# A changed order in the forgetting attention, and ScalarE's function table asked for ahead of two kinds of loops

## What is computed

```python
# forgetting attention: 16 heads of 64, q and k normalised, a decay c added to the logits
q = rms_norm(q.reshape(B, S, FOX_HEADS, FOX_HD), q_g).transpose(0, 2, 1, 3)
k = rms_norm(k.reshape(B, S, FOX_HEADS, FOX_HD), k_g).transpose(0, 2, 1, 3)
log_f = jax.nn.log_sigmoid(fz.astype(f32) + fgate_b.astype(f32))
c = jnp.cumsum(log_f, axis=1).transpose(0, 2, 1)
logits = jnp.einsum('bhqd,bhkd->bhqk', q[:, :, lo:hi], k[:, :, :hi]).astype(f32) * scale
logits = logits + c[:, :, lo:hi, None] - c[:, :, None, :hi]
probs = jax.nn.softmax(jnp.where(mask, logits, -jnp.inf), axis=-1)
outs.append(jnp.einsum('bhqk,bhkd->bhqd', probs.astype(v.dtype), v[:, :, :hi]))
# PEER: the same for all 16384 experts u here, the gates are 0 for those not chosen
act = jax.nn.gelu(jnp.einsum('td,ted->te', ht, u[et]), approximate=False)
return jnp.einsum('te,ted->td', gt * act, v[et])
# feed-forward of the last block
zc = zc + conv_w[tap] * zp[:, tap:tap + S]
gate, val = jnp.split(zc, 2, axis=-1)
return (jax.nn.silu(gate) * val) @ w_down
```

## Time and profile before

| | |
|---|---|
| median of 3 runs | 2532.29 us |
| the profiled execution's own time | 2528.75 us |
| its span, first to last instruction | 2527.0 us |
| TensorE busy | 2401.2 us, 95% |
| VectorE busy | 1634.5 us, 65% |
| ScalarE busy | 1286.7 us, 51% |
| GpSimd busy | 1003.7 us, 40% |
| mean granted clock of TensorE | 0.966 |
| ACT_TABLE_LOAD | 152, of 1.283 us each |

### The profile page before, as it was taken

The page is one execution under the profiler, slowest core; times in us unless marked ns, Lnnn a source line. Parts: engine busy times, 40 slices in busy tenths (PEclk is TensorE's granted clock), DMA queues, the critical chain, the costliest instruction groups (busy, mean ns, idle before and its releaser), DMA issues.

```text
span 2527.0 us, 51551 instructions
## 1 busy us (share of the span) xinstructions
PE 2401.2 (95%) x18346; PEld 2184.2 (86%) x18346; DVE 1634.5 (65%) x3049; ACT 1286.7 (51%) x1698; POOL 1003.7 (40%) x950
## 2 busy tenths in 40 slices
PE   6789999999999999998999989999999999899989
PEld 6779998999988888795899989998888888888987
DVE  5651898677788755422229967778886552334985
ACT  5434555555444444464355555554444544565654
POOL 4526787544333100031278874343330003654330
PEclk9889999999999999996899999999999999999999
DMA  4314555554555566551155545555555664444554
GB/s 145 105 45 142 158 167 165 159 159 157 162 168 165 171 193 196 155 162 42 59 149 175 175 150 166 165 156 165 166 168 177 192 193 141 127 119 134 171 158 150
DMA packets 106103, 383.61 MB, mean 152 GB/s; under 512 B 12433, under 2 KB 12705, under 8 KB 105633
## 3 DMA queue, kind: packets, MB, share of 16 engines
q1 hardware_dynamic: 104400, 379.13, 49.2%
q10 hardware_dynamic: 1616, 3.33, 0.4%
HBM read 381.37 MB, written 1.05 MB: 151 GB/s over the span
## 4 chain that ended last, share of the span: by engine, by line
PE 67%; POOL 14%; issue 13%; DVE 3%; ACT 2%; DVEq 0%; POOLq 0%; ACTq 0%
POOL w_lo L360 13%; PE bank L1565 10%; PE bank L1567 10%; PE bank L1566 10%; PE bank L1476 9%; PE bank L1477 8%; PE bank L1479 8%; PE bank L1739 4%; PE bank L1445 1%; PE bank L1806 1%; PE bank L1811 1%; DVE big L890 1%; ACT w_hi L462 0%; PE bank L1818 0%; PE bank L1638 0%
## 5 line engine op out<-in xcount | busy, mean ns | idle before, releaser
L462 ACT ACTIVATE w_hi<-ring 128x1024 fp32r<-128x1024 f32 x719 | 756.5, 1057 | 715.5 <-PE bank L1567 422.0
L360 POOL TENSOR_TENSOR w_lo<-ring,w_hi 128x1024 fp32r<-128x1024 f32 x281 | 702.6, 2517 | 965.0 <-ACT w_hi L462 963.7
L1476 PE MATMUL bank<-x_hi,w_hi 128*128 128x256 f32 x3328 | 961.3, 289 | 50.8 <-POOL w_lo L360 30.3
L1477 PE MATMUL bank<-x_hi,w_lo 128*128 128x256 f32 x3328 | 947.0, 285 | 0.0
L1479 PE MATMUL bank<-x_lo,w_hi 128*128 128x256 f32 x3256 | 925.8, 284 | 0.0
L855 DVE TENSOR_TENSOR w_lo<-ring,w_hi 128x1024 fp32r<-128x1024 f32 x438 | 539.3, 1232 | 261.1 <-ACT w_hi L462 255.9
L1476 PEld LDWEIGHTS bank<-x_hi,w_hi 128*128 128x128 f32 x3328 | 645.4, 194 | 66.3 <-issue 25.9
L1477 PEld LDWEIGHTS bank<-x_hi,w_lo 128*128 128x128 f32 x3328 | 645.8, 194 | 0.0
L1479 PEld LDWEIGHTS bank<-x_lo,w_hi 128*128 128x128 f32 x3256 | 629.8, 193 | 0.0
L1565 PE MATMUL bank<-w_hi,x_hi 128*128 128x512 f32 x1112 | 440.4, 396 | 5.6 <-DVE x_lo L862 5.6
L1567 PE MATMUL bank<-w_lo,x_hi 128*128 128x512 f32 x1112 | 434.5, 391 | 0.0
(11 more groups left out here) (253 smaller groups left out, 2190.7 us busy)
## 6 DMA issues: line engine op xcount, KB each, us to landing
ring<-u_dram SPq DMA_DIRECT2D x256, 512.0 KB, 3.7
ring<-v_dram SPq DMA_DIRECT2D x256, 512.0 KB, 3.7
ring<-up_dram SPq DMA_DIRECT2D x44, 512.0 KB, 3.7
ring<-wq_dram SPq DMA_DIRECT2D x32, 512.0 KB, 3.6
ring<-sb_in_dram SPq DMA_DIRECT2D x31, 512.0 KB, 3.7
ring<-od_in_dram SPq DMA_DIRECT2D x25, 512.0 KB, 3.6
ring<-down_dram SPq DMA_DIRECT2D x22, 512.0 KB, 3.6
ring<-ev_in_dram SPq DMA_DIRECT2D x21, 512.0 KB, 3.7
```

The source lines that it names most:

```text
L360: pool.tensor_tensor(w_lo[:, k % RING, :], ring[:, k % RING, :], w_hi[:, k % RING, :].bitcast(F32), ALU.subtract).then_inc(g["lo_pool"], 1)
L462: A(w_hi[:, k % RING, :], ring[:, k % RING, :], ACT.Copy).then_inc(g["w_hi_done"], 1)
L1476: mm(dst, hi[:, rows[c]], xh[:, c, :], start=(c == 0), stop=False)
L1477: mm(dst, lo[:, rows[c]], xh[:, c, :], start=False, stop=False)
```

## The change

It has four parts. First, `nc.scalar.preload_act_table` asks for the table set of Gelu in front of each loop of u, and for that of Silu in front of the feed-forward's first unit. Second, the eight slices of q and k are squared, summed and rooted in groups of 3, 3, 2 and 0 instead of 2, 2, 2 and 2. Third, TensorE waits in each `scores(j)` for the slices that this pair reads, where it waited for all eight in front of `fox()`. Fourth, in a pair TensorE turns its two heads ahead of the mix of the pair before, where it mixed first.

```diff
--- before.py
+++ after.py
@@ -48,6 +48,9 @@
 D_FF = 2816
 FC = D_FF // P
 FAR = 1e33
+
+
+SUM_GROUPS = [(0, 1, 2), (3, 4, 5), (6, 7), ()]
 
 
 G_EV, G_PEER0, G_OD, G_PEER1, G_MIX2, G_FFN2 = range(6)
@@ -519,6 +522,8 @@
 
                 loops = units // UNITS
                 highs(n[0] + 2)
+                if func != ACT.Copy:
+                    nc.scalar.preload_act_table(func)
                 if loops:
                     with act.Fori(0, loops) as i:
                         for q in range(UNITS):
@@ -738,11 +743,11 @@
             A(o_z[2], o_z[1], ACT.Ln, bias=1.0).then_inc(g["od_z_log"], 1)
             act.wait_ge(g["units_out"], u[0])
             for j in range(4):
-                for s in (2 * j, 2 * j + 1):
+                for s in SUM_GROUPS[j]:
                     A(o_sq[:, s * 512:(s + 1) * 512], o_qk[:, s * 512:(s + 1) * 512], ACT.Square).then_inc(g["od_sq"], 1)
                 unit(token_major(o_v, D, j), view=lambda s: b3(s, TB))
-                roots([(o_n[:, s * 512:(s + 1) * 512], bank[4 + s % 4][:, :]) for s in (2 * j, 2 * j + 1)], HD,
-                      "od_log", "od_root", 2 * j, "od_sum")
+                roots([(o_n[:, s * 512:(s + 1) * 512], bank[4 + s % 4][:, :]) for s in SUM_GROUPS[j]], HD,
+                      "od_log", "od_root", 3 * j, "od_sum")
             highs(n[0] + 3)
             fox()
             others(8)
@@ -798,6 +803,7 @@
                 A(f_sil[m % 3], f_zc[m % 3][:, 0:T], ACT.Silu).then_inc(g["ff_silu"], 1)
 
             highs(n[0] + 4)
+            nc.scalar.preload_act_table(ACT.Silu)
             z_out(0)
             loops = (FC - 1) // UNITS
             with act.Fori(0, loops) as i:
@@ -1797,6 +1803,7 @@
                 qk = b3(o_n, 16)
 
                 def scores(j):
+                    pe.wait_ge(g["od_qk_ready"], 4 + j // 2 + 1)
                     if j >= 2:
                         pe.wait_ge(g["fox_pt_act"], j - 1)
                         pe.wait_ge(g["fox_pt_dve"], j - 1)
@@ -1841,11 +1848,11 @@
                 for j in range(FH // 2):
                     if j + 1 < FH // 2:
                         scores(j + 1)
+                    turn(2 * j)
+                    turn(2 * j + 1)
                     if j:
                         mix(2 * j - 2)
                         mix(2 * j - 1)
-                    turn(2 * j)
-                    turn(2 * j + 1)
                 back(0)
                 mix(FH - 2)
                 mix(FH - 1)
@@ -1869,10 +1876,9 @@
             one_unit(features, 1)
             for j in range(4):
                 token_unit()
-                for s in (2 * j, 2 * j + 1):
+                for s in SUM_GROUPS[j]:
                     pe.wait_ge(g["od_sq"], s + 1)
                     head_sums(s, o_sq, "od_sum", "od_log")
-            pe.wait_ge(g["od_qk_ready"], 8)
             pe.wait_ge(g["od_bias_ready"], 1)
             pe.wait_ge(g["units_out"], u[0])
             fox()
```

## The result

The changed kernel took 2512.45 us (median of 7 runs, 2503.59 to 2516.38) beside 2527.84 us of the kernel before (7 runs, 2519.72 to 2537.94). The ratio is 0.9931 (95% interval 0.9914 to 0.9949), 17.4 us less (13 to 22), where 12.4 less were forecast; the two medians alone are 15.4 us apart. The sign, the size within the range and the place of most of it came out; two terms of the sum did not.

The account below looks back on a forecast made before the run. TensorE, busy 95% of the span, was taken as the bound. Hand-over 2.4, feed-forward 1, start of fox 3.8, clock 1.5 and turn 3.7 sum to 12.4 us less: 2520 us against the median of 2532.29, range 2496 to 2534.

Parts of the forecast that it names:

- Start of fox: Ahead of fox: regrouped slices leave no root behind the last unit, so TensorE starts 3.8 us earlier (2 to 5.0).
- Clock: In fox: with a smaller gap ahead, first scores run at 2.4 GHz, then it falls; 1.5 us (-1 to 3.8).
- the first rival: In fox: the clock stays up throughout, gaining 21 us in place of 1.5, so 2500 us; chance 0.12.
- the thin start: In fox's first pairs: after two scores TensorE waits for mask and exponential, so the clock was expected to fall early.
- Turn ahead of mix: In fox: a mix covers the 0.74 us wait for turned heads' copies ahead of five scores; 3.7 us (0 to 4.5).
- 2.4 from the hand-over: Hand-over to VectorE in u: nearly a whole table load, 1.2 us, saved once per layer; 2.4 us (0 to 2.6).
- 0 from the rest: Both halves of u: no gain, as VectorE's experts hold the turned slots and TensorE has no gap in the second half.
- The last rival: In u: GpSimd's low parts meet VectorE's two-input operations more often, six more per layer, so 2543 us; chance 0.06.
- Feed-forward: Feed-forward loop: table loads go, but VectorE's convolution and GpSimd's low part need the same time; 1 us (0 to 5.7).
- VectorE doesn't bind: In u and feed-forward: VectorE's chain moves forward with the feed, gaps go, 15.3 us more, 2505 us; chance 0.09.
- the order of fox changes little: In fox: regrouping or turn order brings nothing, only table loads count, about 2529 us; chance 0.10.

Follow-up runs that it names:

- e4: Kernel before with only the turn of a pair put ahead of the mix of the pair before: 2523.76 us, ratio 0.9982.
- e7: Changed kernel with ScalarE's exponentials of the gates after the 28th unit of u instead of the 27th: 2513.99 us, ratio 0.9948 to the kernel before.
- e8: Changed kernel with the gates' exponentials one unit later and TensorE doing 29 units ahead of the turned slots instead of 28: 2506.69 us, ratio 0.9918.
- e5: Kernel before with half of VectorE's 32 products at L1111 left out in each layer: 2518.73 us, ratio 0.9956.
- e6: Changed kernel with half of VectorE's 32 products at L1111 left out in each layer: 2494.95 us, ratio 0.9869 to the kernel before.
- e12: Changed kernel with the third tap of the feed-forward's convolution cut to 8 of 256 columns: 2502.87 us in a single execution.
- e3: Kernel before with only the slice groups of 3, 3, 2 and 0 and the later waits in scores: 2522.06 us, ratio 0.9974.
- e9: Changed kernel with fox's product of q and k over all 128 rows instead of 64: 2518.29 us, ratio 0.9958 to the kernel before.
- e10: Changed kernel with 24 products of bf16 zeros per pair added in fox: 2521.63 us, ratio 0.9970 to the kernel before.

## Why the prediction was right, and where it failed

The time came out within the range, and the term for fox by the mechanism that was forecast. Of the table loads neither term came out: that of u was half of what was measured and put in the wrong place, that of the feed-forward had the wrong sign.

**Start of fox, 3.8 forecast: right, 4.1.** TensorE's position relative to the kernel before was -2.44 us ahead of the sums, so 1154.19 would have been 1151.75, and it is 1147.62. The estimate of 1150.4 for the end of the last unit was 2.9 us too late, of which 2.4 us are the earlier arrival; and into time in which ScalarE waits for the sums fell 0.5 us of the added operations.

**Clock, 1.5: right, 1.5.** From the first scores to the first turn it was 7.5 us and is 5.3, 2.3 less. The rise behind fox takes 0.8 back. The forecast that the clock falls early and stays down held, and so did the reason to give the first rival only 0.12. But the thin start isn't its cause: in the changed kernel the clock fell 3 us after the first scores began, while the first two scores still ran without a gap (5.28 of 5.30 us busy) and before TensorE waited for mask and exponential.

**Turn ahead of mix, 3.7: right, 4.6.** Each of the five waits was worth 0.92 us of the period and not the 0.74 of the idle time that the timeline names. Rows of TensorE that stand back to back overlap (in e4 1163.97 and 1.54 us, and the next row at 1165.31), and rows across a wait don't, so the idle time named in a row is less than what a wait adds to the starts. The prediction should have gone by the starts.

**Sum of fox:** 4.1 + 2.3 + 4.6 - 0.8 = 10.2 us, against 9.0.

**u, 2.4 from the hand-over and 0 from the rest: the size was too small and the place was wrong.** The whole is 5.5 us. The hand-over gave 0.2 us per layer (TensorE's gap of 1.88 us from start to start became 1.70). The chain behind the load at 449.09, GpSimd's two low parts, its copies and VectorE's tables, ended only 0.2 us later than another: VectorE's low parts also wait until ScalarE has taken out a unit that TensorE finishes just then. In the changed kernel that unit binds:

```profile
457.90 0.60 ACT L533 ACTIVATE big<-bank 128x512 f32 x1 [1.91 <-PE bank L1485]
```
```profile
458.72 2.37 DVE L861 TENSOR_TENSOR w_lo<-ring,w_hi 128x1024 fp32r<-128x1024 f32 x2 [0.98 <-ACT big L533]
```

That is 0.22 us from the end of the unit to the low part. Before, the unit was out at 460.78, and the low part started at 461.18, 0.40 us behind it. The prediction had counted a load as being in series with a gap because it stood in front of it. The other 2.5 us per layer are from VectorE's chain, which I had taken as fixed. The last rival named just this mechanism, a GpSimd low part beside a two-input operation, and asked how many meetings there are; it came out with the other sign. The number of low parts from scores to slots is the same, 55, but they lie elsewhere. In layer 0, L1111's 32 products take 50.6 us instead of 54.7, the four comparisons at L1105 13.5 instead of 10.3, and the small steps at L1098 and L1117 1.4 less. VectorE's groups in the same stretch of the changed kernel, where the last line is that of the comparisons:

```profile
L1117 DVE TENSOR_TENSOR sco<-sco,big 128x256 f32<-128x256 f32 x32 | 50.6, 1650 | 0.1
...
L1111 DVE TENSOR_TENSOR sco<-big,iota 128x2048 f32<-128x2048 f32 x4 | 13.5, 3368 | 0.1
```

The groups alone can mislead: in the eight layers without the preload the products take 52.5 to 59.2 us and the comparisons 10.3 to 12.7, but the chains all take 175.5 to 176.4. That one such meeting lengthens the chain by its own price is shown by e7 and e8, that the chain sets TensorE's time by e5 and e6. That meetings also explain the 2.5 us of the preload is argued from these groups. Why just this change of pace is favourable isn't shown: it is where the low parts happen to fall, and the sign was luck. The Trainium skill ("SBUF — State Buffer", section *SBUF: two separate sides*) speaks of such a lock for the whole instruction. The 2.15 us for a low part of about 2.4 agree with it. The 1.28 us for a load and no drain held as well: the exponential at 420.90 starts 1.30 us after the start of its load at 419.60. The 2.66 us of the Trainium skill ("ScalarE: Activation LUTs", section *What ACT_TABLE_LOAD costs*) are not seen.

**Feed-forward, +1: wrong in sign, -0.7.** That VectorE binds was right. What I overlooked is that it then isn't neutral when the low parts come. Each unit has one low part of GpSimd, and it costs VectorE about 2 us wherever it falls: 2.82 us instead of 0.73 at L1388 (now L1394), or 3.81 instead of 1.91 at L1394 (now L1400). VectorE's own operations make some 4.2 us, with the meeting 6.27, and TensorE needs 5.76. Before, the low part fell beside L1394 in two units of three and beside L1388 in the third; two rows of before behind those of the earlier trace rows:

```profile
2404.30 3.87 DVE L1394 SCALAR_TENSOR_TENSOR big<-big 128x256 f32<-128x256 f32 x4 [0.15 <-DVE big L1388]
...
2409.55 2.82 DVE L1388 TENSOR_SCALAR big<-big 128x256 f32<-128x256 f32 x2
```

A meeting at L1394 costs 1.90 or 1.96 us, one at L1388 2.09. Three at L1388, as now, cost 6.27 us and the mix of before 5.95. The difference of 0.32 is the 0.29 by which the three units became longer.

**The rivals.** That VectorE doesn't bind is refuted by e6 and e12: its 15 us are there only when VectorE is relieved, 5.7 us per layer and the 0.63 us per iteration. That the order of fox changes little is refuted by e3 and e4.

The total: 10.2 + 5.5 - 0.7 = 15.0 us by the traces, within the 13 to 22 of the ratio. Between the two profiled executions TensorE is 14.3 us ahead behind the second layer's u and 12.4 at the end; of the 1.9 us that the last block gives back, 0.7 are the feed-forward's, and the rest isn't traced to the change. The forecast's 12.4 had errors of both signs, so that it came close is partly luck.

## What to carry to other kernels

Removing work from an engine that isn't the bound still moves its neighbours in time. Where GpSimd and VectorE share the load, ask which of VectorE's operations GpSimd's next instruction will fall beside, for that decided both terms that I got wrong. A short wait for another engine's last step (0.86 us here) is nearly a tie, and the gain of a faster feed stops there. To see what lies behind the tie, shorten the other chain once, in both kernels. And read the worth of a removed wait from the period of the loop, not from the idle time that stands in front of one instruction.

## What the runs showed of the hardware

- A low part on GpSimd (2.4 to 2.6 us) beside VectorE's products or convolution delays VectorE by 1.9 to 2.15 us (e8), and GpSimd pays as well (two in 5.98 us instead of 4.78, e8). VectorE is delayed also in a TENSOR_SCALAR with two scalars per partition (two of them 0.73 us, and 2.82 with a low part), which has one tensor as input.
- Two products over 64 rows each, in different halves of the rows, run side by side: their four records take 1.23 us at 1.2 GHz, and four over all 128 rows 2.08 (changed kernel and e9).
- TensorE at 1.2 GHz can be busy for 58 of 58 us without the clock's coming back (e9), and the clock can fall in the midst of work with no gap. In e10 it came back after 34 us.
- TensorE's gaps at the turned slots (0.86 + 2.84 us before, 4.07 + 2.17 now) cost some 2 us more behind them, at the lower clock: the next 192 matmuls take 24.6 to 26.0 us, and 23.1 to 23.3 in e5 and e6.
- The spread of a kernel's times (15 to 18 us in 2528) goes along with its mean granted clock, 0.963 to 0.971. A single pair of executions is no measure of a gain of this size.
